# Summing the compressed cache pieces on VectorE instead of TensorE, with another release for the next gather

## What is computed

```python
s16 = kv_cmp.reshape(B, n16, CMP_STRIDE, 2, KVH_D, HD_D).sum(axis=2)
cmp = (s16[:, :-1] + s16[:, 1:]) / CMP_BLOCK
```

## Time and profile before

| | us |
|---|---|
| median of 3 runs | 1435.93 (1435.17 to 1437.82) |
| the profiled execution's own time | 1431.71 |
| its span (first to last instruction) | 1429.9 |

### The profile page before, as it was taken

One profiled execution on the slowest core, in us unless ns is written; L12 is line 12 of the kernel. 1 busy time (PEld: TensorE's weight loads), 2 busy tenths in 40 slices (PEclk: granted clock), 3 DMA queues, 4 the chain that ended last, 5 costly groups with the idle time before them and its releaser, 6 DMA issues.

```text
span 1429.9 us, 24163 instructions
## 1 busy us (share of the span) xinstructions
PE 1294.8 (91%) x10332; PEld 1210.2 (85%) x10332; DVE 618.0 (43%) x893; ACT 394.3 (28%) x615; POOL 500.2 (35%) x262
## 2 busy tenths in 40 slices
PE   4898998999897898888999977799989999999998
PEld 3898997898886887777888855799889999999998
DVE  2544764181425563656667655523054400144102
ACT  3342212022543112223322223322232211222110
POOL 1355432054114334322221234334324434344441
PEclk8799999999998899999999999999989999999999
DMA  4221001533023354431111358322212222222221
GB/s 168 105 89 45 31 31 60 102 95 127 31 87 120 124 179 142 148 104 45 45 60 41 115 190 304 134 75 89 74 59 88 88 89 88 88 90 98 85 94 74
DMA packets 47153, 139.41 MB, mean 97 GB/s; under 512 B 4454, under 2 KB 16074, under 8 KB 46682
## 3 DMA queue, kind: packets, MB, share of 16 engines
q1 hardware_dynamic: 36706, 100.50, 21.4%
q0 software_dynamic: 10368, 37.75, 7.8%
HBM read 129.98 MB, written 8.49 MB: 97 GB/s over the span
## 4 chain that ended last, share of the span: by engine, by line
PE 74%; DVE 11%; DMA 5%; ACT 3%; issue 3%; POOL 2%; DVEq 0%; ACTq 0%
PE PS L598 41%; PE PS L806 9%; PE PS L626 7%; DMA M<-cache_cmp_kv,idx 3%; PE PS L678 3%; PE PS L953 2%; DMA M<-cache_slc_kv,idx 2%; POOL WL L2050 1%; DVE tmp L1427 1%; PE PS L940 1%; PE PS L969 1%; PE PS L584 1%; PE PS L1005 1%; PE PS L769 1%; PE PS L713 1%
## 5 line engine op out<-in xcount | busy, mean ns | idle before, releaser
L2050 POOL TENSOR_TENSOR WL<-M,WH 128x1024 fp32r<-128x1024 f32 x159 | 389.1, 2450 | 784.2 <-ACT WH L1139 783.8
L1139 ACT CAST WH<-M 128x1024 fp32r<-128x1024 f32 x159 | 165.8, 1046 | 389.1 <-DMA M<-weights 389.1
L598 PE MATMUL PS<-hH,WH 128*128 128x260 f32 x1040 | 217.5, 291 | 20.1 <-DVE hL L1431 18.2
L598 PE MATMUL PS<-hL,WH 128*128 128x260 f32 x1040 | 213.3, 287 | 0.0
L598 PE MATMUL PS<-hH,WL 128*128 128x260 f32 x1040 | 213.3, 287 | 0.0
L598 PEld LDWEIGHTS PS<-hH,WH 128*128 128x128 f32 x1040 | 164.5, 194 | 25.6 <-issue 10.1
L598 PEld LDWEIGHTS PS<-hL,WH 128*128 128x128 f32 x1040 | 164.5, 193 | 0.0
L598 PEld LDWEIGHTS PS<-hH,WL 128*128 128x128 f32 x1040 | 164.5, 193 | 0.0
L806 PE MATMUL PS<-hH,WH 128*128 128x260 f32 x384 | 114.8, 299 | 4.5 <-ACT tmp L1287 2.6
L806 PE MATMUL PS<-hL,WH 128*128 128x260 f32 x384 | 110.4, 288 | 0.0
L806 PE MATMUL PS<-hH,WL 128*128 128x260 f32 x384 | 110.2, 287 | 0.0
(11 more groups left out here) (370 smaller groups left out, 2433.0 us busy)
## 6 DMA issues: line engine op xcount, KB each, us to landing
M<-weights SPq DMA_DIRECT2D x159, 512.0 KB, 3.7
M<-cache_win_kv POOLq DMA_DIRECT2D x7, 512.0 KB, 5.3
spill<-xT SPq DMA_DIRECT2D x1, 2080.0 KB, 9.6
M<-spill SPq DMA_DIRECT2D x1, 2080.0 KB, 8.6
M<-x_prompt SPq DMA_DIRECT2D x4, 512.0 KB
y_prompt<-M SPq DMA_DIRECT2D x4, 512.0 KB
con<-tables SPq DMA_DIRECT2D x1, 1437.5 KB, 12.2
M<-state_gla SPq DMA_DIRECT2D x2, 512.0 KB, 6.8
```

Of the source, the lines that this page charges most:

```text
L598: last = mm(PS[:, bank + h, 0:HALF], w[:, slot_of(n), k, :], x[:, HALF * h:HALF * h + HALF], start=(start and k == k0 and w is WH and x is ...
L1139: nc.scalar.copy(WH[:, at].rearrange("p k n -> p (k n)"), WR[:, at]).then_inc(sem("w_hi"), 1)
L2050: p.tensor_tensor(WL[:, at].rearrange("p k n -> p (k n)"), WR[:, at], WH[:, at].rearrange("p k n -> p (k n)"), ALU.subtract).then_inc(sem( ...
```

## The change

DVE adds the pieces of a sample up. For each piece it adds columns 0 to 511 and 512 to 1023 out of the gather's buffer into another place: for the first piece of a sample into `total`, for the others into `part`, which it then adds to `total`. After the fourth piece it folds `total` to 256 columns and raises `c_fold`. `total` and `part` are the two halves of the `masks` constant and change roles with each sample. A new semaphore `c_free` is raised by the first addition of each piece; gather q waits for it to reach q - 1, and so does the later stage's first gather for 32. PE makes one product per sample, after k = 5, 11, 17, ... 47.

```diff
+        CSAMPLES = (4, 5, 6, 7, 0, 1, 2, 3)
+        CSUM = [C("masks", 512 * i, 512 * i + 512) for i in range(2)]
...
-                if k % 3 == 2 and k < 48:
-                    for q in (2 * (k // 3), 2 * (k // 3) + 1):
-                        compressed_sum(q)
+                if k % 6 == 5 and k < 48:
+                    compressed_sum(k // 6)
...
-                pe.wait_ge(sem("c_fold"), q + 1)
-                if q and q % 8 == 0:
-                    pe.wait_ge(sem("sh_ev"), q // 8)
-                mm(PS[0:NCMP, 5, 256 * (x % 2):256 * (x % 2) + 256], C("shift", 0, NCMP), W3[q % 2][:, 0:256],
-                   start=(c == 0), stop=(c == 3)).then_inc(sem("c_mm"), 1)
+                pe.wait_ge(sem("c_fold"), n + 1)
+                if n and n % 2 == 0:
+                    pe.wait_ge(sem("sh_ev"), n // 2)
+                mm(PS[0:NCMP, 5, 256 * (x % 2):256 * (x % 2) + 256], C("shift", 0, NCMP), CSUM[n % 2][:, 0:256],
+                   start=True, stop=True).then_inc(sem("c_mm"), 1)
...
                     for q in (2 * (k // 3), 2 * (k // 3) + 1):
+                        n, c = q // 4, q % 4
+                        total, part = CSUM[n % 2], CSUM[1 - n % 2]
+                        w = W3[q % 2]
                         dve.wait_ge(sem(f"xc{q % 2}"), 16 * (q // 2 + 1))
-                        w = W3[q % 2]
-                        step(v.tensor_tensor(w[:, 0:512], w[:, 0:512], w[:, 512:1024], ALU.add))
-                        v.tensor_tensor(w[:, 0:256], w[:, 0:256], w[:, 256:512], ALU.add).then_inc(sem("c_fold"), 1)
+                        if c == 1 and n:
+                            dve.wait_ge(sem("c_mm"), n)
+                        v.tensor_tensor(part if c else total, w[:, 0:512], w[:, 512:1024], ALU.add).then_inc(sem("c_free"), 1)
+                        dve.wait_ge(sem("c_free"), q + 1)
+                        if c:
+                            step(v.tensor_tensor(total, total, part, ALU.add))
+                        if c == 3:
+                            v.tensor_tensor(total[:, 0:256], total[:, 0:256], total[:, 256:512], ALU.add)\
+                                .then_inc(sem("c_fold"), 1)
...
-                    dve.wait_ge(sem("c_mm"), 8 * (k // 12) + 8)
+                    dve.wait_ge(sem("c_mm"), 2 * (k // 12) + 2)
...
-                    gp.wait_ge(sem("c_mm"), q - 1)
+                    gp.wait_ge(sem("c_free"), q - 1)
...
-                    gp.wait_ge(sem("c_mm"), len(CPIECES))
+                    gp.wait_ge(sem("c_free"), len(CPIECES))
```

More of the change, by code:

```diff
@@ L374, in build @@
         W3 = [R[:, 12416 + 3072:12416 + 4096], R[:, 16512 + 3072:16512 + 4096]]
-        CPIECES = [(x, c) for x in (4, 5, 6, 7, 0, 1, 2, 3) for c in range(4)]
+        CSAMPLES = (4, 5, 6, 7, 0, 1, 2, 3)
+        CPIECES = [(x, c) for x in CSAMPLES for c in range(4)]
+        CSUM = [C("masks", 512 * i, 512 * i + 512) for i in range(2)]
         XR = W3 + [C("masks"), zu[:, 0:1024], zu[:, 1024:2048], zg[:, 0:1024], zg[:, 1024:2048]] \
@@ L808, in mix_step, with compressed_sum @@
                 last.then_inc(sem("prod"), 1)
-                if k % 3 == 2 and k < 48:
-                    for q in (2 * (k // 3), 2 * (k // 3) + 1):
-                        compressed_sum(q)
-            def compressed_sum(q):
-                x, c = CPIECES[q]
-                pe.wait_ge(sem("c_fold"), q + 1)
-                if q and q % 8 == 0:
-                    pe.wait_ge(sem("sh_ev"), q // 8)
-                mm(PS[0:NCMP, 5, 256 * (x % 2):256 * (x % 2) + 256], C("shift", 0, NCMP), W3[q % 2][:, 0:256],
-                   start=(c == 0), stop=(c == 3)).then_inc(sem("c_mm"), 1)
+                if k % 6 == 5 and k < 48:
+                    compressed_sum(k // 6)
+            def compressed_sum(n):
+                x = CSAMPLES[n]
+                pe.wait_ge(sem("c_fold"), n + 1)
[3 more added lines that the diff above has]
+                   start=True, stop=True).then_inc(sem("c_mm"), 1)
             def mix_steps(a, b):
```

## The result

The changed kernel takes 1438.81 us (median of 9 runs, 1437.70 to 1439.75), the kernel before in the same comparison 1433.59 (9 runs, 1430.36 to 1437.82): ratio 1.0035, 95% interval 1.0021 to 1.0049, so **slower by 5.0 us**, 0.35%. A second comparison gave 1440.12 against 1435.83, ratio 1.0033 (1.0016 to 1.0049). The forecast was 1435.5 and no difference that can be measured; the time lies 0.3 us above the range. (The forecast started from 1435.93, the median of the first three runs; counted from 1433.59 it would be 1433.2.) The profiled execution took 1438.66 us, with a span of 1436.9.

A forecast was written before the change was run, and what follows sets the result against it. The prediction took PE's order, lengthened by its waits, as the bound. Gains and delays walked product by product left PE 0.4 us ahead at k = 47, so 1435.5 us against the median of 1435.93; range 1431.2 to 1438.5.

The forecast's parts named there:

- The bound: Whole program: PE's order, lengthened by its waits; line 819 kept PE idle 21.1 us, all behind DVE's fold.
- third rival: DVE's longer additions meet POOL more often: stalls grow from 12.2 to 14.4 us, 2.2 more, giving 1437.7; chance 0.10.
- The tail: DVE's work behind a sample's last landing grows from 1.15 to 1.86 us, adding 0.7 us at each of 8 remaining waits.
- k = 5: First sum: landing behind POOL's subtraction as before, longer DVE work after it, PE ending near 463.1 against 462.44; -0.7 us.
- lead: How much earlier than in the kernel before PE stands at a given point, in us; negative means later.
- k = 11: Second sum: DVE's addition and fold still follow POOL's subtraction, PE through at 490.7 against 489.8 before; -0.9 us.
- the walk: Product-by-product estimate of PE's gain or delay from k = 5 to k = 47, ending 0.4 us ahead.
- k = 14 and 16: PE's 2.85 us wait at k = 14 goes; k = 16 waits for its bank until 498.4 instead of starting at 501.5; +3.1.
- the term for the clock: At k = 23, a 3.4 us wait lowers PE's clock, costing 1.5 us (ends 0 and 3.1), leaving +0.8 of +2.3.
- the steps to k = 29, 41 and 47: Sums whose gathers stand behind POOL's subtraction: PE ahead by 0.2, 1.1 and 0.4 us there.
- second rival: Fewer but longer waits lower PE's clock at k = 11, 23 and 41: 1.5 to 4.7 us more, 1437 to 1440; chance 0.13.
- first rival: Gains of k = 16 (3.1) and k = 32 to 36 (1.6) both last: 1431.2, at most 9.0 us, 1426.9; chance 0.20.

The follow-up runs named there:

- e2_release: The kernel before with only the new gather release (first addition into the constant's halves), PE keeping four products per sample: 1433.12 us, ratio 0.9975 to the kernel before.
- e1_warm: The changed kernel with spare matmuls filling PE's long waits, also ahead of k = 16: 1433.25 us, ratio 0.9980 to the kernel before.
- e7_warm_tail: The changed kernel with the last piece folded alone (short tail) and spare matmuls ahead of its waits and k = 16: 1426.69 us, ratio 0.9950 to the kernel before.
- e12_change_again: The changed kernel unaltered, timed and profiled a second time: 1440.12 us, ratio 1.0033 to the kernel before.
- e8_warm_k5: The changed kernel with spare matmuls at k = 5 alone: 1439.11 us, ratio 1.0042 to the kernel before.
- e5_warm_before: The kernel before with spare matmuls ahead of its waits at k = 5, 14, 29 and 47: 1430.55 us, ratio 0.9980 to the kernel before.
- e4_tail: The changed kernel with three pieces folded ahead, the last folded alone and two accumulating products per sample: 1435.87 us, ratio 1.0009 to the kernel before.
- e3_late: The changed kernel with PE's sum two products later, DVE's additions left in place: 1433.31 us, ratio 0.9976 to the kernel before.
- e6_warm_release: The kernel before with the new gather release alone, plus spare matmuls ahead of its four long waits: 1426.19 us, ratio 0.9956 to the kernel before.
- e11_change_shift: The changed kernel with DVE's additions, PE's sum and the copy behind it one product later, long tail kept: 1420.68 us, ratio 0.9913 to the kernel before.

## Why the prediction was wrong

- **The bound** was read rightly: PE's order, with PE's waits for DVE's fold in it. The release did what was said: in the kernel after (440 to 632 us), POOL's gathers no longer wait for PE, but 23.1 us for line 1671, in place of 37.0 for line 819. That was off the critical path at most places, and released alone (e2_release) it was worth 0.25%.
- **The third rival falls.** DVE's groups by line, kernel after, 440 to 632 us, answer to the earlier trace rows:

```profile
L1671 DVE TENSOR_TENSOR con<-M 128x512 f32<-128x512 f32 x32 | 26.5, 828 | 21.0 <-DMA M<-cache_cmp_kv,idx 20.3
L1674 DVE TENSOR_TENSOR con<-con 128x512 f32<-128x512 f32 x24 | 18.7, 778 | 0.8
...
L1676 DVE TENSOR_TENSOR con<-con 128x256 f32<-128x256 f32 x8 | 3.4, 426 | 0.3
```

  The additions took 26.5 + 18.7 + 3.4 = 48.6 us, 6.5 over the 42.1 of the medians; before it was 12.2 over 35.7. More addition time met fewer stalls, not 2.2 us more of them. The Trainium skill's rule (SBUF — State Buffer, section "Who interferes with whom") may hold for the single addition, as at k = 10 before, but it doesn't say how often the two engines meet, and that followed from the order here.
- **The tail**: 0.7 us at each of eight waits, 5.6 in all, was the right kind and near the right size: short against long it measured 3.7 us, and 4.3 with the clock held (6.8 by the stretches of e1_warm and e7_warm_tail). PE stood at five of the eight.
- **k = 5** (lead -0.7; measured 0.0, and -1.1 in e12_change_again) and **k = 11** (-0.9; -0.35 and +1.4) were within 0.7 us in the first profile, by luck in part, since the second is off by 2.3 at k = 11. But the wait at k = 11, one of those that the prediction listed as a sign of being right, was in neither: PE reached it no earlier than DVE, since it had run at half clock before it (462.6 to 469.4 and 476.2 to 486.5 us). With k = 5 covered it waited there, 1.84 us in e1_warm and 2.08 in e8_warm_k5. The first long wait had a price, 1.22 us for the pair and half clock behind it, which the walk carried as in the kernel before.
- **The step that failed is "k = 14 and 16: here the wait goes ... Lead +3.1", and with it the term for the clock, one fall of 1.5 us at k = 23.** From k = 11 to the start of k = 16 the walk gains 4.0 us. The bank of k = 16 waits for `mix_mul` behind the additions, as the prediction said, and PE stood there for 3.42 us (3.43 in e12_change_again):

```profile
503.17 0.36 PE L808 MATMUL PS<-hH,WH 128*128 128x260 f32 x1 [3.42 <-DVE xT L1657]
```

  The wait that the change took away at k = 14 had come back two products later, and the clock fell behind it as it had at k = 14: 0.66 over 503 to 508 us, where the kernel before has 1.00 for the same products. PE began k = 16 with a lead of +0.8 (+2.6 in e12_change_again) and ended it with -0.7 (+1.1): 1.5 us went in this one product, in both profiles, and the walk had them at nothing. Its own numbers held the wait. It has k = 14 end at 496.95 - 2.85 = 494.1 before; with its 0.9 us of delay and the 1.6 us that k = 15 takes at full clock PE stands at k = 16 from 496.6 to the 498.4 of its bank, an estimate of 1.8 us that it didn't price.
- **The other part of k = 16** is one of the first profile alone: the bank came 2.4 us later than forecast there, 0.5 in e12_change_again. A fall from 476.2 us lasted 10.3 us, where the kernel before and e12_change_again have 6.8 at that place. Windows of the kernel after and, under it, of the kernel before (the end of 64 small matmuls at line 858, before 857, then k = 9 and in the kernel before the start of k = 10):

```profile
476.00:486.50 10.50, 10.50 (x55) 10.44 (x54) 5.30 (x7) 1.24 (x2) 0.00 (x0) 0.51 0.07 25
```

```profile
473.80:484.00 10.20, 10.20 (x64) 10.13 (x64) 5.58 (x6) 1.54 (x2) 0.00 (x0) 0.67 0.16 56
```

  POOL's subtraction came 2.0 us later by it, and the gather of piece 8 2.3.
- **The price of a fall was right, the number of falls wrong.** Behind k = 23 the lead went from -2.3 at the end of the sum to -4.3 at the end of k = 26, so 2.0 us (1.6 in e12_change_again) where 1.5 was chosen between 0 and 3.1. Behind k = 41 it went from -4.0 to -5.5 at the end of k = 42, 1.5 in both profiles, where the forecast has nothing and only its upper end, 1437, a fall. From k = 16 to the sum of k = 23 another 1.6 us (2.4) went in place of 0.8; the steps to k = 29, 41 and 47 were within 0.3 of the walk's. In the kernel before the clock fell behind the waits at k = 5, 14, 29 and 47, after at 5, 16, 23, 29, 41 and 47. Behind k = 29 and 47, where waits of 3.63 and 2.98 us grew to 5.76 and 5.24, it was at half no longer than before (6.8 to 6.9 us each).
- With the clock held the lead at k = 47 is +1.3 in e1_warm, and the forecast without its 1.5 would be +1.9. That this is so near is partly luck: the spare matmuls also took falls away that the walk had carried over from the kernel before. Against e5_warm_before, where they are gone too, the lead is -0.7.
- The mechanism was thus the **second rival**, with 0.13 of the chance, in part: of its three places k = 23 and 41 came and k = 11 did not, and the fall of k = 14, which it took off, moved to k = 16. It has 1.1 to 4.3 us over the kernel before, and 5.0 were measured; its 1437 to 1440 holds 1438.81 by the higher median that it started from. The tail and PE's order (e4_tail, e3_late) have a part of their own that it doesn't name. That the length of one wait decides, from a point between 1.48 and 2.85 us, the other runs don't bear out: in e6_warm_release the clock fell to 0.50 right behind 1.16 us at k = 41, in e11_change_shift it stayed at 1.00 behind 2.62. For each, the wait in the timeline and the window behind it:

```profile
589.07 0.71 PE L830 MATMUL PS<-con 128*127 128x256 f32 x2 [1.16 <-DVE con L1681]
589.60:593.00 3.40, 3.40 (x17) 2.94 (x16) 1.05 (x3) 0.81 (x4) 0.23 (x1) 0.50 0.87 287
```

```profile
579.51 0.30 PE L941 MATMUL PS<-con,M 128*128 128x128 f32 x1 [2.62 <-DVE M L1889]
579.50:583.00 3.50, 3.46 (x27) 3.31 (x28) 1.58 (x5) 0.82 (x5) 1.30 (x2) 1.00 0.62 178
```

- **The first rival**, that the gains add up, has its time in e11_change_shift, at 0.87% even beyond its bound of 9.0 us. The clock didn't fall there behind the sum of k = 23, which was one of its two conditions; it needed PE and DVE one product later, and not shorter landings (median 5.2 us, 5.3 before).

How the fall at 476 us starts was not settled. No long wait ends there; PE is 3.6 us into 64 small matmuls of 32 columns each, which follow one another without a gap:

```profile
472.62 8.16 PE L858 MATMUL PS<-stat,M 64*128 64x32 f32 x64
```

It stands in the kernel before too (at 473.8) and in e1_warm, e5_warm_before and e8_warm_k5, so the spare matmuls at other places didn't remove it. The falls at k = 16, 23 and 41 are priced above by the products behind them; what each cost the whole program was not separated. e8_warm_k5, the one try, showed that covering k = 5 alone changes nothing. Holding the clock, a short tail and a later sum each take the loss away or nearly so, so it can't be dealt out among them.

## What to carry to other kernels

When a change gathers several short waits of TensorE into fewer long ones, price each new wait twice: its idle time, and the products behind it at half the clock, by rows of such waits, and then ask whether those products lead to the next landing. Look also for a wait that only moves: ask what the engine meets next when one is gone. Work taken off the bounding engine shows only if its next wait can't take it: move the consumer, and the producer's order with it, later until the removed time appears as time and not as idle time. To find out whether the clock is the cause, fill the waits with spare matmuls: if the granted clock stays up behind them and added work makes the kernel faster, it is, at least in part.

## What the runs showed of the hardware that was not expected

Added work can buy time: 180 spare matmuls, 22.1 us of busy PE, shortened the stretch by 7.0 us. In e1_warm PE's waits of 0.74 to 1.84 us behind the spare matmuls left the clock at 1.00; behind 2.79 us at k = 47 it fell, as behind every wait of 2.80 us and over at the sums of the kernel after. Other runs show that the length of one wait doesn't settle it: a fall behind 1.16 us in e6_warm_release, none behind 2.62 in e11_change_shift. The clock also fell where PE's matmuls followed one another without a gap, 3.6 us into the small matmuls of line 858 (0.51 over 10.5 us from 476 us), so a full PE row in the busy digits is no sign of full clock.

The Trainium skill says (TensorE: Matmul & The Clock Gate, section "Loop structure matters more than you think") that a long wait for a transfer between matmuls lets PE's clock drop, so that the matmuls behind it run slow, and that dense matmuls keep it up. These traces agree, with 0.55 behind 5.04 us of waiting and 1.00 where the wait was filled, though the wait here was for DVE's additions behind the transfer; the fall at 476 us, in small matmuls without a gap, is one that the section doesn't name.
